# A 32-bit two-block transformer kernel: the feed forwards' up projections by Strassen's scheme

## The reference

```
def swiglu_2(h, w1, w3, w2):
    return (jax.nn.silu(h @ w1) * (h @ w3)) @ w2
...
h = x * (1.0 + sc_f) + sh_f
x = layer_norm(ALPHA * x + g_f * swiglu_2(h, ffn_w1[i], ffn_w3[i], ffn_w2[i]), ln_g[i, 1], ln_b[i, 1])
```

## Time and profile before

| what | value |
|---|---|
| median of 3 runs | 4054.96 us (4053.62 to 4080.22) |
| profiled execution, its own time | 4054.95 us |
| its span, first to last instruction | 4052.3 us |
| PE busy | 3794.8 us (94%) |
| PEld busy | 3138.7 us (77%) |
| DVE, ACT, POOL busy | 1373.0, 1249.8, 1260.1 us (34%, 31%, 31%) |
| mean granted clock of TensorE | 0.951 of full |

### The profile page before, as it was taken

The page is one execution under the profiler, slowest core; times in us unless marked ns, Lnnn a source line. Parts: engine busy times, 40 slices in busy tenths (PEclk is TensorE's granted clock), DMA queues, the critical chain, the costliest instruction groups (busy, mean ns, idle before and its releaser), DMA issues. The chain is left out here.

```text
span 4052.3 us, 76771 instructions
## 1 busy us (share of the span) xinstructions
PE 3794.8 (94%) x32494; PEld 3138.7 (77%) x32494; DVE 1373.0 (34%) x2758; ACT 1249.8 (31%) x2182; POOL 1260.1 (31%) x658
## 2 busy tenths in 40 slices
PE   6998999999899999989799999989999989989997
PEld 5877788888777677768698888768888868667785
DVE  3345211111444211175557775251111150643111
ACT  3234311121346322232234443231112142643222
POOL 2201222222334343332233432122222223634442
PEclk8999999999999999999879999999999989999998
DMA  4232232332200434332201100133233112012221
GB/s 175 69 107 100 89 124 89 111 107 83 74 5 32 160 136 166 135 108 107 82 21 30 28 22 24 63 120 110 77 114 130 52 52 74 23 48 86 96 85 71
DMA packets 118121, 342.82 MB, mean 85 GB/s; under 512 B 33103, under 2 KB 39759, under 8 KB 117455
## 3 DMA queue, kind: packets, MB, share of 16 engines
q1 hardware_dynamic: 117839, 338.73, 24.1%
HBM read 323.88 MB, written 16.93 MB: 84 GB/s over the span
## 5 line engine op out<-in xcount | busy, mean ns | idle before, releaser
L204 POOL TENSOR_TENSOR feed_low<-ring,feed_high 128x1024 fp32r<-128x1024 f32 (+1 forms) x236 | 620.5, 2629 | 1324.1 <-ACT feed_high L197 1292.1
L221 PE MATMUL ps<-hn_high,feed_high 128*128 128x512 f32 x2016 | 717.7, 356 | 9.3 <-DVE h L1231 5.1
L221 PE MATMUL ps<-hn_low,feed_high 128*128 128x512 f32 x2016 | 714.4, 354 | 0.0
L221 PE MATMUL ps<-hn_high,feed_low 128*128 128x512 f32 x2016 | 713.2, 354 | 0.0
L221 PEld LDWEIGHTS ps<-hn_high,feed_high 128*128 128x128 f32 x2016 | 381.1, 189 | 91.2 <-issue 24.6
L221 PEld LDWEIGHTS ps<-hn_high,feed_low 128*128 128x128 f32 x2016 | 381.0, 189 | 53.4
L221 PEld LDWEIGHTS ps<-hn_low,feed_high 128*128 128x128 f32 x2016 | 381.2, 189 | 51.4
L1400 DVE TENSOR_TENSOR ps<-feed_gate,ps 128x768 f32<-128x768 f32 (+1 forms) x88 | 73.0, 829 | 969.2 <-PE ps L221 949.2
L197 ACT ACTIVATE feed_high<-ring 128x1024 fp32r<-128x1024 f32 (+1 forms) x240 | 272.7, 1138 | 365.8 <-PE ps L221 365.7
L221 PE MATMUL ps<-feed_hid_high,feed_high 128*128 128x512 f32 (+1 forms) x1056 | 379.7, 360 | 0.0
L221 PE MATMUL ps<-feed_hid_high,feed_low 128*128 128x512 f32 (+1 forms) x1056 | 376.7, 357 | 0.0
(11 more groups left out here) (592 smaller groups left out, 7429.3 us busy)
## 6 DMA issues: line engine op xcount, KB each, us to landing
feed_side_ring<-in_ada SPq DMA_DIRECT2D x144, 512.0 KB, 5.7
ring<-in_ffn_g SPq DMA_DIRECT2D x88, 512.0 KB, 3.5
ring<-in_ffn_u SPq DMA_DIRECT2D x88, 512.0 KB, 3.5
ring<-in_ffn_d SPq DMA_DIRECT2D x64, 704.0 KB, 4.1
diff_side_ring<-in_ada SPq DMA_DIRECT2D x32, 512.0 KB, 4.2
ring<-in_od_in SPq DMA_DIRECT2D x24, 512.0 KB, 3.4
ring<-in_ev_in SPq DMA_DIRECT2D x23, 512.0 KB, 4.3
ring<-in_even_in SPq DMA_DIRECT2D x20, 512.0 KB, 3.8
```

Of the source, the lines that this page charges most:

```text
L204: pool.tensor_tensor(self.low[:, j % self.slots, 0:w], feed.ring[:, slot, 0:w], self.high[:, j % self.slots, 0:w].bitcast(F32), ALU.subtra ...
L221: mm = pe.matmul(dst, weights[a], values[b], start=first and n == 0, stop=last and n == 2)
```

## The change

It replaces the up projections' scheme and with it the whole order of the feed forward. What is left out of the diff is marked.

For each hidden chunk n the gate tile and the up tile are one 2 by 2 block matrix: gate rows a11, a12 and up rows a21, a22, each with 512 of the 1024 input features. The activations are a 2 by 2 block matrix too: features 0 to 511 and 512 to 1023, first and second half of the tokens (384 or 256 columns). Seven block products (four feature chunks, three parts: twelve matmuls each) take the place of eight, with four sums of weights per chunk (s1 = a21+a22, s2 = s1−a11, s3 = a11−a21, s4 = a12−s2) and four sums of activations per stage (t1 to t4, `CrossedStream.cross`), all on VectorE, and the products are put together by seven additions of VectorE per chunk.

```diff
+RING_SLOTS = 5
+RING_FLOATS = 5632
...
     def ffn(g, u, d):
-        return [part for h in range(2) for part in (
-            ("feed_up_first", 1, [(0, g, 0, HALF * h), (1, u, 0, HALF * h)]),
-            ("feed_up", HALF // 2, [((2 + 2 * p + m) % 4, w, 2, HALF * h + 1 + p) for p in range(2) for m, w in enumerate((g, u))]),
-            ("feed_down", 2, [(s, d, 4, KC * h + s) for s in range(4)]))]
+        down = d.rearrange("(h n) p (c w) -> h c p n w", h=2, w=P)
...
+        return ("feed", 1, [(j % RING_SLOTS, source[kind](n), None, 0) for j, (kind, n) in enumerate(FEED_TILES)])
...
+def operand_order():
+
+    order = [("a11", 0), ("a12", 0), ("a11", 1), ("a12", 1)]
+    for n in range(FC):
+        order += [("s2", n), ("s1", n), ("s3", n)]
+        if 1 <= n < FC - 1:
+            order += [("a11", n + 1), ("a12", n + 1)]
+        order += [("a22", n), ("s4", n)]
+        if n >= 2 and n % 2 == 0:
+            order += [("down", 2 * n - 4 + j) for j in range(4)]
+    return order + [("down", 2 * FC - 4 + j) for j in range(4)]
...
+class Operands:
...
+    SLOTS = 6
...
+    def write_high(self, act, e):
...
+        if e >= self.SLOTS:
+            act.wait_ge(self.products, e - self.SLOTS + 1)
...
+    def write_low(self, pool, e):
...
+        pool.tensor_tensor(self.low[:, slot, :], self.source(name, n), self.high[:, slot, :].bitcast(F32), ALU.subtract).then_inc(self.low_ready, 1)
+        if name in ("a22", "s4") or name == "down" and n % 4 >= 2:
+            released = "a12" if name == "s4" else name
+            pool.drain()
+            pool.sem_inc(self.k.feed.used[self.k.feed.count(self.k.feed.at, self.tile(released, n))[0]], 1)
+
+    def add_three(self, dve, n):
+
+        self.wait_raw(dve, "a11", n)
+        self.wait_raw(dve, "a22", n)
...
         @st.block.tensor
         def _(pe):
+            def product(name, n, values):
+
+                p = PRODUCT_AT[name, n]
+                if p >= 4:
+                    before, m = PRODUCTS[p - 4]
+                    if before == "a11":
+                        pe.wait_ge(s1_ready, m + 1)
+                    else:
+                        wait_taken(pe, before, m)
...
+            norm.tensor(pe)
+            first_two()
+            for n in range(FC):
+                middle(n)
+                if next_c:
+                    sm.accumulate(pe, 4 + 2 * n)
+                if 1 <= n < FC - 1:
+                    first(n + 1)
+                last(n)
+                if next_c:
+                    sm.accumulate(pe, 5 + 2 * n)
+                if n >= 2 and n % 2 == 0:
+                    down(n // 2 - 1)
...
         @st.block.scalar
         def _(act):
...
+            for n in range(FC):
+                after("s2", n)
+                if n:
+                    put_hidden(n - 1)
...
         @st.block.vector
         def _(dve):
...
+            for n in range(FC):
+                first, second = slice(0, H), slice(H, tokens)
+                if n:
+                    put_low(n - 1)
+                if n + 1 < FC:
+                    operands.add_three(dve, n + 1)
+                operands.wait_product(dve, "s2", n)
+                dve.tensor_tensor(u2[:, :], s1[:, :], bank("s2", n), ALU.add).then_inc(taken, 1)
```

725 lines of the change are left out of this document (498 added, 227 removed).

## The result

The changed kernel takes 4516.70 us (median of four runs, 4506.26 to 4771.02) against 4067.59 us of the kernel before beside it: ratio 1.109, 95% interval 1.102 to 1.117. The highest of the four is a disturbed run and is not in the ratio. The profiled execution took 4506.26 us, 451 more than the one shown of before; forecast were 350 more.

The account below looks back on a forecast made before the run. TensorE's columns were taken as the bound, every wait before it paid in full. Chain 166 us (128 us gain counted), clock 76, ports 20, front 70, tail and scaling 18: 350 on 4054.95, so 4405 us; range 4210 to 4530.

Parts of the forecast that it names:

- Products and side tiles: Up projections: matmuls of 384 columns 0.174 us, of 256 0.120; lone side tile 1.08 us; fewer columns gain 128 us.
- The chain: Turns 2 to 20: s2, low part of s4, up tile's load, sums, reading s2, then a12; +166 us, gain included.
- Issue to landing of 512 KB, 3.4 us: Step of the chain, followed in D: the up tile's load takes 3.4 us from SyncE's issue to landing.
- The clock: TensorE's clock falls to half behind the waits in B and D: 76 us (0 to 95).
- For the 38 waits of B and D I take 2.0 us each: Clock step: each wait in B and D costs 2.0 us through the lowered clock, 76 us in all.
- The ports: VectorE's operations with two SBUF operands wait for GpSimd; in even turns of B and D 20 us (0 to 60).
- GpSimd's low parts against crossings of two SBUF operands bring, I estimate, 1 and 4 more: At the stage's front: GpSimd's low parts beside VectorE's crossings add 1 us in A and 4 in B.
- Front and tail: Stage fronts +70 us (30 to 100), tails +10, scaling of `h` in C and D +8.
- Turns 0 and 1: First turns of each stage, counted without the wait; scaling of `h` fills them in C and D, +8 us.
- The loads are not late: Rival, chance 0.10: the up tile lands early enough that the chain never ends last; 4085 us, within 1%.
- VectorE is the bound: Rival, chance 0.10: VectorE's sums, readings, residuals and port waits fill a turn of D; 88 turns 1.7 us longer, 4555 us.
- The wait without its echo: Rival, chance 0.17: the chain is there, but neither clock nor port adds; 4309 us.

Follow-up runs that it names:

- the run with the added matmuls: Changed kernel, in stage D alone 32 unused matmuls of 256 columns added between products a11 and a12 of a chunk: 4470.61 us, 1.101 to before.

## Why the prediction was right, and where its sizes were off

Direction, place and chain were right, and the time lay in the range, near its upper end. Point by point, with 350 us forecast and 451 measured:

| term | forecast | measured |
|---|---|---|
| two turns of A, C, without the down phase; forecast without falls of the clock | 37.1 | 39.4 and 40.6, with them |
| two turns of B, without the down phase, with two falls of the clock | 36.1 | 36.7 |
| two turns of D, the same | 33.3 | 33.7 |
| matmul of 384 and of 256 columns | 0.174, 0.120 | 0.173, 0.119 |
| side tile alone | 1.08 | 1.08 |
| first scaling to `middle(0)` in A, in B | 31, 20 | 47.4, 30.1 |
| turns 0 and 1 together, A to D | 34, 24, 38, 24 | 40.0, 31.5, 47.2, 39.3 |

- **Products and side tiles** were right to 0.001 and 0.01 us. That two lone tiles could share the four quadrants at the price of one was not seen.
- **The chain** was right in its links. Its length, from the start of s2 to a12 over turns 3 to 19, was right in odd turns (11.6, 11.2, 11.6 and 11.1 us in A to D for 11.5, 11.3, 11.5 and 11.0) and too short in even ones (11.8, 11.0, 12.1 and 10.5 for 10.8, 10.0, 10.8 and 9.7). The step too small was "Issue to landing of 512 KB, 3.4 us": beside the other loads it takes 4.2 to 4.7 us in A and C and 3.6 to 3.8 in D. That the odd turns of A and C came out in spite of it is luck: the 0.7 us for GpSimd's two low parts in front did not come, its low part of s4 ends 4.4 us behind s2's start in both kinds of turn.
- **The clock** had about the right sum in the wrong place. The step that failed is "For the 38 waits of B and D I take 2.0 us each", and nothing for A and C. A fall makes D's three products from a12 on about 1.5 us longer (5.9 us in odd turns, 4.4 where the clock held). In the odd turns that is hidden in the next wait (the run with the added matmuls), in the even ones it costs some 1.5 us, which rests on two turns, and in A and C 1.5, 8 times in A and 13 in C in the first profile. If B's odd turns hide it as D's do, which was not tried, that is by this estimate 15+15+12+20 = 62 us instead of 76. That B's and D's pairs in the table came out within 0.6 us is partly luck: a chain too short and falls priced too high nearly cancel.
- **The ports.** In the turns the term was small, as long as the load was late. It was large at the front: "GpSimd's low parts against crossings of two SBUF operands bring, I estimate, 1 and 4 more" is the worst-sized step. VectorE's low parts cost 4.77 us per pair instead of 1.6, and 10.50 for the last two pairs together, 20.0 us in A instead of 6.4.
- **Front and tail.** With that, with the first four side tiles (3.3 us in A), which had no price, and with 4.5 us of matmuls at the lower clock behind the last low part, the front, from the first scaling on, was forecast some 13 us too short in A and C and 3 in B and D. The sum in the prediction has a slip besides: 26 and 4 us are 30, not 31.
- **Turns 0 and 1** were taken as free of waits, with 8 us for the scaling in C and D together. They are 6, 7, 10 and 15 us longer. In D four chunks of the scaling take VectorE 7.5 us in turn 0 (5.80 and 1.67), between silu·up of one chunk and the reading of s2 of the next.

Set together: turns 2 to 20 are 22 us over the forecast in A and 33 in C, and, with the port's 20 us counted, 9 under it in B and D together; turns 0 and 1 are 38 over it. What is left of the 101 us, front, last turn and tail together, is 10 over in A and in C each, 3 under in B and 1 under in D. The fronts alone are over 30 too short in the forecast, so the last turn and the tail must have been forecast too long, by 15 us or more; that was not traced.

Of the rivals, "The loads are not late" named the point that decides, the operand whose low part frees the slot. Its time was 4085, though, and freeing the slot early gives 4263: behind the load stood "VectorE is the bound", with the contention as its reason. Both were true in B and D, one behind the other, and the prediction had priced them as alternatives. "The wait without its echo" (4309) was right in D's odd turns and false in A, where a fall of the clock costs its full length.

## What to carry to other kernels

Count what a scheme with fewer products adds to the engines that feed it, and ask of each wait what it hides: here, on 512 tokens, a late load hid a contention of ports, which hid TensorE's own limit, and three small edits (who frees a slot, where the sums stand, two side tiles side by side) were worth 430 us. An eighth fewer products must carry the scheme's front, first turns and tail. Here it does with 768 tokens and doesn't with 512, and it does least where VectorE has other work in the first turns.
